# The last FFN's up projection by seven products of quarters instead of eight, with kept splits of the down weights and an earlier output projection

## The reference, cut to what matters

```python
def swiglu(h, w_up, w_down):
    g, u = jnp.split(h @ w_up, 2, axis=-1)     # w_up: 1024 x 5632
    return (jax.nn.silu(g) * u) @ w_down       # w_down: 2816 x 1024
```

## Time and profile before

| | |
|---|---|
| median of 3 runs | 2446.63 us (2445.74 to 2449.91) |
| profiled execution | 2445.97 us, its span 2444.2 us |
| PE busy | 2420.0 us, 99% of the span |
| POOL / DVE / ACT busy | 1180.9 / 988.5 / 875.2 us |
| DMA | 335.91 MB, mean 137 GB/s |
| last FFN of B | from about 2054 us to the end |

### The profile page before, as it was taken

How to read it: one execution, slowest core, us unless ns; L and a number is a source line. 1 busy time by engine, 2 the same in 40 slices (tenths; PEclk the granted TensorE clock), 3 DMA queues, 4 the chain that set the end, 5 groups by cost and what they waited for, 6 DMA issues and landing times.

```text
span 2444.2 us, 37585 instructions
## 1 busy us (share of the span) xinstructions
PE 2420.0 (99%) x15528; PEld 2187.7 (90%) x15528; DVE 988.5 (40%) x1712; ACT 875.2 (36%) x1154; POOL 1180.9 (48%) x933
## 2 busy tenths in 40 slices
PE   9999999999999999999999999999999999999998
PEld 6899987787888988999999989988888889999998
DVE  4513246344445344433343434344443434323324
ACT  5431235343223355433333243254432324222223
POOL 3722147655555444635445550064455555554454
PEclk9999999999999999999999999999999999999999
DMA  9863363322324587322223274432232344222222
GB/s 326 308 224 138 143 249 124 127 70 78 117 78 136 175 277 265 124 78 87 87 70 104 92 275 167 160 97 78 78 126 94 113 151 142 87 95 96 88 86 87
DMA packets 102249, 335.91 MB, mean 137 GB/s; under 512 B 12288, under 2 KB 16192, under 8 KB 102080
## 3 DMA queue, kind: packets, MB, share of 16 engines
q1 hardware_dynamic: 102080, 333.52, 39.9%
HBM read 255.20 MB, written 76.16 MB: 136 GB/s over the span
## 4 chain that ended last, share of the span: by engine, by line
PE 90%; DVE 3%; POOL 3%; issue 1%; ACT 1%; POOLq 1%; DMA 1%; DVEq 0%; SPq 0%; ACTq 0%
PE ps L830 64%; PE ps L896 19%; POOL wl L1466 2%; POOLq L1472 1%; PE ps L936 1%; PE ps L992 1%; PE ps L990 1%; PE ps L912 0%; PE ps L1053 0%; PE ps L1050 0%; PE ps L996 0%; PE ps L947 0%; POOL rsA L1478 0%; POOL sq L1573 0%; DMA wr<-in_wblk 0%
## 5 line engine op out<-in xcount | busy, mean ns | idle before, releaser
L1466 POOL TENSOR_TENSOR wl<-wr,wh 128x512 fp32r<-128x512 f32 x656 | 869.1, 1353 | 592.1 <-ACT wh L1196 588.6
L830 PE MATMUL ps<-xh,wh 128*128 128x260 f32 (+2 forms) x3296 | 881.1, 322 | 5.2 <-DVE xA L1860 2.2
L830 PE MATMUL ps<-xl,wh 128*128 128x260 f32 (+2 forms) x3296 | 867.7, 318 | 0.0
L830 PE MATMUL ps<-xh,wl 128*128 128x260 f32 (+1 forms) x3280 | 866.1, 319 | 0.0
L830 PEld LDWEIGHTS ps<-xh,wh 128*128 128x128 f32 (+1 forms) x3296 | 543.1, 187 | 59.5 <-issue 17.0
L830 PEld LDWEIGHTS ps<-xl,wh 128*128 128x128 f32 (+1 forms) x3296 | 542.5, 187 | 44.7 <-issue 2.4
L830 PEld LDWEIGHTS ps<-xh,wl 128*128 128x128 f32 x3280 | 540.9, 188 | 44.4
L1196 ACT ACTIVATE wh<-wr 128x1024 fp32r<-128x1024 f32 (+1 forms) x332 | 343.4, 1046 | 380.5 <-DMA wr<-in_wblk 376.3
L896 PE MATMUL ps<-hidh,wh 128*128 128x260 f32 (+1 forms) x1024 | 275.2, 322 | 3.7 <-DVE hf L1873 1.4
L896 PE MATMUL ps<-hidl,wh 128*128 128x260 f32 (+1 forms) x1024 | 274.2, 321 | 0.0
L896 PE MATMUL ps<-hidh,wl 128*128 128x260 f32 (+1 forms) x1024 | 272.9, 320 | 0.0
(11 more groups left out here) (375 smaller groups left out, 2288.9 us busy)
## 6 DMA issues: line engine op xcount, KB each, us to landing
wr<-in_wblk SPq DMA_DIRECT2D x328, 512.0 KB, 3.7
split<-wh SPq DMA_DIRECT2D x64, 512.0 KB, 5.4
split<-wl SPq DMA_DIRECT2D x64, 512.0 KB, 6.4
wh<-split SPq DMA_DIRECT2D x64, 512.0 KB, 3.2
wl<-split SPq DMA_DIRECT2D x64, 512.0 KB, 4.2
xr<-in_xT SPq DMA_DIRECT2D x8, 260.0 KB, 6.4
xB<-in_xT SPq DMA_DIRECT2D x8, 260.0 KB, 5.4
out_yT<-xB SPq DMA_DIRECT2D x8, 260.0 KB, 2.2
```

The source lines that it names most:

```text
L830: mm = pe.matmul(ps[0:cols, b + c, 0:n], wt[:, w], xt[:, e:e + n], start=first, stop=end)
L1466: last = pool.tensor_tensor(lo[:, e], raw[:, e], hi[:, e].bitcast(F32), ALU.subtract)
```

## The change

Three things change in layer 1, and one in every stage.

1. The up projection of the last FFN (B) works on quarters. For each hidden tile `f` (22 of them) the weights are a 2 x 2 matrix of pieces, each 128 x 512: gate or up, by first or second half of the contraction (`a11, a12, a21, a22`). The activations are split the same way in contraction and tokens, 260 tokens each. DVE makes four sums of weight pieces, and seven products of 4 tiles of contraction each (three matmuls per tile, 84 in all) replace two units of 48. The norm's factor is now multiplied into the activations ahead of the products (`scaled`), which also drops L1637, L1573 and L1873 there. Two sets of buffers hold the pieces of even and odd `f`. ACT writes the high parts (3584 columns), POOL the low parts of all seven pieces, in place, after DVE's sums of that set are all made.
2. The splits of layer 1's down blocks are stored to HBM in A's FFN (22 blocks) and read back in B's (`down_blocks`, four transfers of 512 KB a group, issued when the group's slots come free).
3. `out(1, B)` moves ahead into A's FFN, behind the up units of group 8; B's last norm, the activation quarters and the first weight set are made during A's groups 8 to 10. Samples and mixes go one group sooner. A's final norm moves into B's FFN (`nrm 8` at f = 18, `fin` at f = 19 and 21).
4. POOL writes the low part of a normal block with one instruction of 1024 columns instead of two of 512.

```diff
+PIECE = (0, 3, 1, 4, 5, 6, 7)
+PSTEP = (0, 1, 0, 2, 2, 3, 3)
+XPIECE = (0, 2, 1, 3, 4, 5, 6)
+PAIRS = ((0, 2), (3, 4), (4, 6), (6, 8))
...
+    def last_ffn(at):
+        for f in range(NF):
+            g, kk = f // 2, f % 2
+            for i in range(7):
+                add(("sp", f, i))
+                if i == 1 and f and (kk or f == 2):
+                    add(("hl", 1, B, (f - 1) // 2, (f - 1) % 2))
+                if i == 2 and f + 2 < NF:
+                    add(("wq", f + 2))
+                for s in at.get((f, i), ()):
+                    add(s)
+            add(("hh", 1, B, g, kk))
...
+            if kk and g:
+                for m in range(KT):
+                    add(("down", 1, B, g - 1, m))
+                    if m == 1:
+                        add(("hl", 1, B, g, 1))
...
+                if g + 1 < NG:
+                    add(("wd", g))
...
+                           (8, 1): mix(1, B)[0:2], (8, 2): mix(1, B)[2:4], (8, "end"): outs,
+                           (8, "down", 2): [("nrm", LAST)], (8, "down", 3): [("nrv", LAST)],
...
+                           (10, "down", 2): [("xl", 4)], (10, "down", 3): [("wH", 0, 2), ("wP", 0, 2)],
+                           (10, "down", 5): [("wH", 0, 3), ("wP", 0, 3)], (10, "down", 6): [("xl", 5)],
+                           (10, "down", 7): [("wq", 1)], (NG, "down", 2): [("xl", 6)], (NG, "down", 4): [("wH", 1, 0), ("wS", 1, 0)],
+                           (NG, "down", 6): [("wH", 1, 1), ("wS", 1, 1)], (NG, "down", 7): [("wd", 0)]}))
...
+            put(f - 1, (0,), ("wS", f, 0))
+            put(f - 1, (2,), ("wS", f, 1), ("wP", f, 0), ("wP", f, 1), ("wH", f, 2))
+            put(f - 1, (3,), ("wP", f, 2), ("wH", f, 3))
+            put(f - 1, (4,), ("wP", f, 3))
...
+            put(f - 1, (0,), ("wS", f, 0))
+            put(f - 1, (3,), ("wS", f, 1))
+            put(f - 1, (5,), ("wH", f, 2), ("wP", f, 0), ("wP", f, 1))
+            put(f - 1, (6,), ("wH", f, 3), ("wP", f, 2))
+            put(f - 1, ("down", 2), ("wP", f, 3))
...
+def product_bank(f, i):
+    x, y, z = banks_of(f // 2)
+    one, two = (y, z) if f % 2 else (x, y)
+    return (2 * one + 1, 2 * one, 2 * one + 1, 2 * two + 1, 2 * two, 2 * one, 2 * one + 1)[i]
...
+            def first_product(it, f):
+                act.wait_ge(s_unit, pl.u[it] + 1)
...
+                act.activation(p1[f % 2][:], ps[:, pl.bank[pl.u[it]], 0:Q], ACT.Copy).then_inc(s_eva, 1)
+            def gate_sum(f):
+                act.wait_ge(s_evd, pl.evac["sp", f, 5])
+                act.activation(gsum[:], gsum[:], ACT.Silu).then_inc(s_gsi, 1)
...
-                for e in (slice(0, w // 2), slice(w // 2, w)):
-                    last = pool.tensor_tensor(lo[:, e], raw[:, e], hi[:, e].bitcast(F32), ALU.subtract)
-                last.then_inc(s_lo, 1)
+                pool.tensor_tensor(lo, raw, hi.bitcast(F32), ALU.subtract).then_inc(s_lo, 1)
...
+            def set_lo(f, j):
+                pool.wait_ge(s_qhi, 4 * f + j + 1)
+                pool.wait_ge(s_wsum, f + 1)
+                for n in range(*PAIRS[j]):
+                    e = slice(512 * n, 512 * n + 512)
+                    last = pool.tensor_tensor(wql[f % 2][:, e], wqr[f % 2][:, e], wqh[f % 2][:, e].bitcast(F32), ALU.subtract)
+                last.then_inc(s_qlo, 1)
...
+            def set_sums(f, part):
+                if part == 0:
+                    v.wait_ge(s_wq[f % 2], 32 * (f // 2 + 1))
+                    v.tensor_tensor(s1, a21, a22, ALU.add)
+                    v.tensor_tensor(s3, a11, a21, ALU.subtract)
+                else:
+                    v.tensor_tensor(s2, s1, a11, ALU.subtract)
+                    v.drain()
+                    v.tensor_tensor(s4, a12, s2, ALU.subtract).then_inc(s_wsum, 1)
...
+            def products_sum(it, f, i):
+                if i < 2:
+                    return
...
+                if i == 2:
+                    v.tensor_tensor(gsum[:, 0:Q], part, u1, ALU.add).then_inc(s_evd, 1)
+                elif i == 3:
+                    v.tensor_tensor(u1, part, u1, ALU.add).then_inc(s_evd, 1)
+                    v.drain()
+                    v.tensor_tensor(p4[:], ps[:, pl.bank[pl.u["sp", f, 1]], 0:Q], u1, ALU.add).then_inc(s_evd, 1)
+                elif i == 4:
+                    v.tensor_tensor(t5[:], part, u1, ALU.add).then_inc(s_evd, 1)
+                elif i == 5:
+                    v.tensor_tensor(gsum[:, Q:2 * Q], part, t5[:], ALU.add).then_inc(s_evd, 1)
+                else:
+                    v.tensor_tensor(hf[:, t:t + Q], part, p4[:], ALU.add)
+                    v.tensor_tensor(hf[:, t + Q:t + 2 * Q], part, t5[:], ALU.add).then_inc(s_evd, 1)
+                    v.drain()
+                    v.wait_ge(s_gsi, f + 1)
+                    v.tensor_tensor(hf[:, t:t + 2 * Q], hf[:, t:t + 2 * Q], gsum[:], ALU.mult).then_inc(s_hm, 1)
```

More of the change, by code:

```diff
@@ L84, in ffn @@
                     add(("nrm", N_FFN[L, X]))
+            for s in at.get((g, "end"), ()):
+                add(s)
             if g:
@@ L87, in ffn @@
                     add(("down", L, X, g - 1, m))
+                    for s in at.get((g, "down", m), ()):
+                        add(s)
                     if m == 1:
@@ new lines, in order, with down_block, banks_of @@
+    for m in range(KT):
+        put(2 * m + 3, ("down", 5), ("xs", 8, m))
+    put(18, (0,), ("nrm", 8), ("nrv", 8))
+    for m in range(KT):
+        put(19 + 2 * (m // 4), ("down", 2 * (m % 4)), ("fin", m))
+        if m % 2:
+            put(19 + 2 * (m // 4), ("down", 2 * (m % 4)), ("fo", m - 1))
+    last_ffn(at)
+    return it
+def down_block(g):
+    return NB + B_FFN + (8 + g * 6 if g < NG - 1 else 4 + (NG - 1) * 6)
+def banks_of(g):
+    return (0, 1, 2) if g % 2 == 0 else (1, 0, 2)
+def product_bank(f, i):
+    x, y, z = banks_of(f // 2)
+    one, two = (y, z) if f % 2 else (x, y)
+    return (2 * one + 1, 2 * one, 2 * one + 1, 2 * two + 1, 2 * two, 2 * one, 2 * one + 1)[i]
@@ L289, in __init__ @@
                 self.rs_end[x[1]] = rs_cur[NORMS[x[1]][0]]
-            if k not in ("sm", "in", "z", "out", "up", "down", "dh", "rg", "s1"):
+            if k not in ("sm", "in", "z", "out", "up", "down", "dh", "rg", "s1", "sp"):
                 continue
@@ L301, in __init__ @@
             b = cur % 4
-            cur += nb
+            if k == "sp":
+                b = product_bank(x[1], x[2])
+            elif k == "down" and x[1:3] == (1, B):
+                b = 2 * banks_of(x[3] + 1)[(0, 2, 1)[x[4] % 3]]
+            else:
+                cur += nb
             self.u[x] = u
@@ L327, in __init__ @@
                 new = [NB * x[1] + B_FFN + (0 if g == 0 else 4 + (g - 1) * 6) + q]
[L328 to L334, removed]
-                        src_end[n] = u
-                    self.blk[u] = down["dh"]
+            elif k in ("sp", "dh") or k == "down" and x[1:3] == (1, B):
+                continue
             elif k == "down":
@@ L380, in __init__ @@
         self.again = [n for n in self.second if self.second[n]]
-        self.kept = [n for n, s in enumerate(self.blocks) if not self.second[n] and not isinstance(s, tuple) and s % NB < B_FFN]
+        downs = {down_block(g) + i for g in range(NG) for i in range(2)}
+        self.kept = [n for n, s in enumerate(self.blocks)
+                     if not self.second[n] and not isinstance(s, tuple) and (s % NB < B_FFN or s in downs)]
         self.loads, self.splits, self.stores, at, split = {}, {}, {}, [0] * 4, 0
@@ L396, in __init__ @@
                 items.append(("ws", x[1] - 2))
+            if x == ("w", len(self.blocks) - 1):
+                items.extend(("ws", n) for n in (x[1] - 1, x[1]) if n in kept)
         self.items = items
@@ L777, in _ @@
                     final_half(v[0])
-            for s in range(4):
-                sp.wait_ge(s_ws[s], pl.stores[len(pl.blocks) - 4 + (s - len(pl.blocks)) % 4])
             sp.wait_ge(s_st0, 16)
@@ L1031, in gla_sample_end @@
                     pe.wait_ge(s_q2, 1)
-                    pe.matmul(ps[:, 5, 64:128], ones, osq[:], start=True, stop=True).then_inc(s_qm2, 1)
+                    pe.matmul(ps[:, 5, 64:128], ones, osq[:], start=True, stop=True).then_inc(s_qm, 1)
             def mlstm_columns(X):
@@ L1407, in _ @@
                     x_first_square(v[0])
+                elif k == "lnw":
+                    act.activation(vb[:, 0:1], pcol("eps"), ACT.Ln)
+                elif k == "xh":
+                    quarter_hi(v[0])
+                elif k == "wH":
+                    set_hi(*v)
+                elif k == "sp" and v[1] == 0:
+                    first_product(it, v[0])
+                elif k == "sp" and v[1] == 5:
+                    gate_sum(v[0])
                 elif k == "xe":
```

303 lines of the change are left out of this document (238 added, 65 removed), and 7 rows, old and new, of the table outs.

## The result

The changed kernel takes 2451.35 us (2448.35 to 2454.32, 20 runs), the kernel before 2446.64 us (2443.75 to 2450.5, 20 runs): ratio 1.0019, 95% interval 1.0013 to 1.0025. The forecast was 2431.

A forecast was written before the change was run, and what follows sets the result against it. PE's matmul stream was taken as the bound: 2445.97 - 31.7 (matmuls removed) + 13 (waits in the last FFN) + 3 (A's FFN) = 2430.3 us profiled, so a median of 2431; range for 8 in 10, 2417 to 2446.

The forecast's parts named there:

- Term 1: Last FFN: 264 matmuls removed from PE at 0.120 us each, 31.7 us gained; a group without waits 31.8 us.
- Term 2: Last FFN: PE waits as DVE and POOL take turns, 1.3 us a group, 13 us over ten groups.
- collision doubled: Rival, last FFN: multiply misses its slot, 26 us lost, A's FFN costs 6; 2447 us, no change; chance 0.14.
- Term 3: A's FFN: DVE's added work fits on average but is close in the downs; 3 us lost, from 0 to 10.
- Parts at nothing: Single-instruction low part 0 (-1 to +3), stores of 22 blocks 0 to 2 us; ACT's added work loses nothing on the path.
- The late raw set: Rival, last FFN: raw weight set lands late behind down splits, DVE held 3.5 us a group; 2466 us; chance 0.10.
- What I said would show it: Last FFN: groups about 33 us, PE waits about 1 us on DVE sums in odd tiles only, 264 matmuls fewer.

The follow-up runs named there:

- e8: The changed kernel with e7's moved weight sums and e4's later hidden high part together: 2426.26 us, ratio 0.9920 to the kernel before.
- e1: The changed kernel with the low part of a normal block again in two POOL instructions of 512 columns: 2447.53 us, ratio 1.0007 to the kernel before.
- e3: The kernel before with only the splits of layer 1's down blocks stored in A's FFN and read back in B's: 2446.34 us, ratio 1.0004.
- e5: The changed kernel with POOL's low parts of the last FFN's weight quarters replaced by zero fills: 2432.06 us, ratio 0.9946 to the kernel before.
- e11: e9 with the low part of a normal block in one POOL instruction of 1024 columns: 2424.90 us, ratio 0.9909 to the kernel before.
- e9: e8 with normal blocks' low part in two pieces, the A-to-B hand-over spread out, a later wait for A's final factor: 2419.86 us, ratio 0.9892.
- e7: The changed kernel with DVE's weight sums at other places in its queue: 2433.79 us, ratio 0.9951 to the kernel before.
- e4: The changed kernel with ACT's copy of product 0 ahead of its hidden high part, for even tiles: 2449.18 us, ratio 1.0014 to the kernel before.
- e10: e1 with the work at the hand-over from A's FFN to B's spread out, order of sums kept: 2445.21 us, ratio 0.9994 to the kernel before.

## Why the prediction was wrong

- **Term 1 was right.** 264 matmuls fewer; a group without waits takes 31.7 us in e8 against 31.8 forecast, 12 matmuls of one bank are 1.43 to 1.44 us. The gain of 31.7 us is there in full.
- **Term 2 is the step that failed, by its size.** The mechanism was as followed: DVE instructions with both operands in SBUF take turns with POOL's, product 2 waits for ACT's copy and product 5 for DVE's sums. I took 1.3 us a group; it was 2.2. It also fell in other places: I had 0 in the even tile, 0.2 ahead of the odd tile's product 2 and 1.1 ahead of its product 5, and PE lost 0.65, 1.14 and 0.35 there. Three things are in that (times from the even tile's first matmul, 2152.04):
  - The multiply missed its slot. I had it ask at 11.1, with POOL's fourth part over at 11.4. POOL started at 2158.77 (6.7), so four parts of 1.26 end at 11.8, and the multiply came at 11.8 too (2163.81 - 2152.04); it lost to the fifth part and was over at 2165.61, 13.6 and not 12.0. This is the rival "collision doubled", whose condition was a margin of 0.3 us; I gave it 0.14. The even tile's own wait had pushed DVE's last sums from 11.1 to 11.7 (2163.71).
  - The even tile has a wait, where I had none. I let product 3's sums end at 7.1 with the bank due at 7.2, and priced this margin of 0.1 at nothing; they ended at 7.6 (2159.66). Dependent sums start 0.52 apart, with a drain between them that I had left out; two without one start 0.34 apart (2162.95 and 2163.29). The rest of the half microsecond is small errors in the steps ahead of them.
  - A break costs PE 0.2 us more than its idle time (0.65 for 0.42, 1.14 for 0.91).
- **Term 2 also left out the first group.** I counted ten groups of one pattern. Tiles 0 to 3 have no downs between them, so no 11.6 us in which POOL and DVE catch up, and the even tile 2 pays for the lateness of tile 1: an idle time of 2.62 us and the lower clock behind it. They lost 8.7 us against my 1.3. The steady groups lost 20.4 against 11.7, of which 1.6 stand at f = 18, for which I had 1 in term 3: 0.9 are the two matmuls of A's norm, 0.7 a longer wait (PE is idle for 1.14 us there, not 0.42).
- **Term 3 was too small:** 7.8 us to B's first product instead of 3, inside my bounds of 0 to 10. The average fits, as I said; the last eight downs do not. PE was never idle in this stretch before and is idle for 6.5 us after: 2.2 ahead of B's first product, 2.7 in A's last downs (part 4, by e1), 1.1 for POOL's sums of B's norm, which I had not priced, and 0.5 in two short ones. The clock I hadn't priced at all; its two stretches, 1.6 us each, are in the 8.7 of the first tiles.
- **Parts at nothing.** Part 2 and the raw sets: right (e3; no wait of DVE or PE on a DMA in B's FFN). Part 4: I gave 0, from -1 to +3, and it is some 3 to 4 us (0.0012 and 0.0017 in two pairs, each with overlapping intervals, and 0.0008 alone on the kernel before): at the far end. My argument that DVE waits longer but more rarely fails where DVE has no slack. The late raw set did not come about.
- **What I said would show it** came in part: 264 matmuls fewer, weight sums of 1.6 to 1.8 us in odd tiles and 0.69 in even ones, no wait on POOL's low parts or on the raw set. The rest did not: a group takes 33.9 us and not about 33, even tiles have a wait too, and the list names ACT for both, where I had DVE's sums. My range's upper end, 2446, was the doubled collision at 2447, which I had priced at 6 us for A's FFN and nothing for the first tiles. With 29.1 us lost after the first product and 7.8 before it, the change gives back more than the 31.7 it takes out.

The Trainium skill, SBUF — State Buffer, § Who interferes with whom, has it that a DVE instruction with two SBUF inputs contends with a POOL instruction that reads SBUF, and not with one that only writes it. e5 agrees: in the third tile, with POOL writing but not reading at the same time, the multiply takes 0.70 us instead of 1.66.

## What to carry to other kernels

When an engine is at its bound, a change that takes out its work pays only if every hand-over around it keeps its margin; follow one period by hand on every engine, and where a margin is under the error of your durations (here 0.3 us), price both outcomes at even chances. Follow the first period too, since it lacks the pauses of the steady one. Before giving up such a change, move the added work: the same instructions in other places of the list made 0.2% slower into 0.9% faster (e11), and into 1.1% with part 4 undone (e9).

## What the runs showed of the hardware

- POOL instructions that only write (fills, 0.53 us for 128x512) held no DVE instruction in e5's third tile (0.70 and 0.69 us); those that read two operands make 0.70 into up to 1.80 us. POOL's own part goes from 1.26 us to 9.68/7 = 1.38 with DVE's between.
- An idle PE can lower the clock for what follows. The same idle time of 2.18 us ahead of B's first product was followed by matmuls at 0.50 in the change and by matmuls at 1.00 in e8 (first two products, windows of 2.0 and 3.4 us). Elsewhere 2.08 (e7), 2.31 (e4), 2.81 (e1) and, in the third tile, 2.62 us (the change, e1, e4 and e10) were followed by 0.50, while 1.56 us in A's downs and 1.64 us ahead of B's first product (e5) left it at 1.00. So an idle time of 2 us may cost 2 or 3.6 us; what decides was not settled. The Trainium skill, TensorE: Matmul & The Clock Gate, Part 1, has it that the same kernel can meet the gate at another phase from run to run; the change and e8 are two kernels, so they fit with that and do not prove it.
